# Decoder block on one core: the first normalisation's scale and offset applied to transposed tiles, the last output tile shared by three engines

## The reference

```python
h = layer_norm(x, ln0_g, ln0_b)            # (x - mean) * rsqrt(var + eps) * g + b
proj = jnp.einsum('bsd,dn->bsn', h, w_in[i])
...
h = layer_norm(DEEPNORM_ALPHA * h + mix, ln1_g[i], ln1_b[i])
...
h = layer_norm(DEEPNORM_ALPHA * h + ff + ple, ln2_g[i], ln2_b[i])
```

## Time and profile before

| what | value |
|---|---|
| median of 3 runs | 1636.98 us (1636.86 to 1637.41) |
| the profiled execution | 1637.65 us, span 1635.8 us |
| PE, PEld busy | 1588.1 us (97%), 1325.1 us (81%) |
| VectorE, ScalarE, GpSimd busy | 1150.4 (70%), 744.0 (45%), 694.2 (42%) |
| chain that ended last | PE 83%, VectorE 5%, ScalarE 4%, DMA 2%, GpSimd 2% |
| DMA | 208.51 MB, mean 127 GB/s |
| first slice of 40.9 us | PE 6 tenths, DMA 8 tenths, 295 GB/s; all later slices of PE but the last at 8 or 9 |

### The profile page before, as it was taken

One profiled execution on the slowest core, in us unless ns is written; L12 is line 12 of the kernel. 1 busy time (PEld: TensorE's weight loads), 2 busy tenths in 40 slices (PEclk: granted clock), 3 DMA queues, 4 the chain that ended last, 5 costly groups with the idle time before them and its releaser, 6 DMA issues.

```text
span 1635.8 us, 21111 instructions
## 1 busy us (share of the span) xinstructions
PE 1588.1 (97%) x7800; PEld 1325.1 (81%) x7800; DVE 1150.4 (70%) x1724; ACT 744.0 (45%) x1162; POOL 694.2 (42%) x487
## 2 busy tenths in 40 slices
PE   6999999999999999999999989999999999999996
PEld 4888888888888887888887868888888888888886
DVE  8558878437767668656336879986666579857977
ACT  3245454327888774511233644445444553433342
POOL 5222221522333145564443597765566323223334
PEclk9999999999999999999999999999999999999999
DMA  8211110101010143521333435554444598867672
GB/s 295 77 42 38 27 39 27 39 29 38 27 53 27 39 117 97 147 78 52 122 120 118 164 126 183 182 195 143 159 168 152 185 330 254 272 199 238 194 204 104
DMA packets 220693, 208.51 MB, mean 127 GB/s; under 512 B 9000, under 2 KB 190504, under 8 KB 218544
## 3 DMA queue, kind: packets, MB, share of 16 engines
q1 hardware_dynamic: 217424, 196.09, 38.7%
q10 hardware_dynamic: 3168, 11.08, 1.7%
HBM read 160.96 MB, written 46.17 MB: 127 GB/s over the span
## 4 chain that ended last, share of the span: by engine, by line
PE 83%; DVE 5%; ACT 4%; DMA 2%; POOL 2%; issue 2%; SPq 0%; DVEq 0%; ACTq 0%; POOLq 0%
PE dense L969 7%; PE dense L971 7%; PE dense L973 7%; PE dense L979 4%; PE dense L1315 3%; PE dense L1317 3%; PE dense L1316 3%; PE dense L1395 3%; PE dense L1396 3%; PE dense L1397 3%; PE mixA L1106 2%; PE dense L1047 2%; PE dense L1049 2%; PE dense L1048 2%; PE mixA L1315 2%
## 5 line engine op out<-in xcount | busy, mean ns | idle before, releaser
L969 PE MATMUL dense<-parts 128*128 128x512 f32 x528 | 183.3, 409 | 1.6 <-DVE page L2090 0.9
L943 POOL TENSOR_TENSOR parts<-page,parts 128x512 fp32r<-128x512 f32 x52 | 88.9, 1733 | 208.1 <-ACT parts L1909 208.1
L862 POOL TENSOR_TENSOR parts<-page,parts 128x512 fp32r<-128x512 f32 x108 | 156.3, 1469 | 44.9 <-ACT parts L1788 41.6
L971 PE MATMUL dense<-parts 128*128 128x512 f32 x528 | 174.0, 391 | 0.0
L973 PE MATMUL dense<-parts 128*128 128x512 f32 x528 | 173.3, 390 | 0.0
L854 POOL CAST parts<-page 128x1024 fp32r<-128x1024 f32 x43 | 49.3, 1145 | 287.4 <-PE dense L973 192.4
L905 POOL TENSOR_TENSOR page<-page 128x512 f32<-128x512 f32 x80 | 122.6, 1532 | 59.8 <-PE dense L1317 25.2
L913 POOL TENSOR_TENSOR parts<-page,parts 128x512 fp32r<-128x512 f32 x80 | 114.8, 1437 | 55.4 <-ACT parts L1835 50.6
L1919 ACT CAST parts<-page 128x1024 fp32r<-128x1024 f32 x56 | 58.8, 1055 | 142.8 <-DVE page L2614 123.2
L973 PEld LDWEIGHTS dense<-parts 128*128 128x128 f32 x528 | 99.1, 188 | 21.8
L971 PEld LDWEIGHTS dense<-parts 128*128 128x128 f32 x528 | 99.1, 188 | 21.0
(11 more groups left out here) (298 smaller groups left out, 4315.8 us busy)
## 6 DMA issues: line engine op xcount, KB each, us to landing
page<-in_w_ff SPq DMA_DIRECT2D x104, 512.0 KB, 6.0
page<-in_w_in SPq DMA_DIRECT2D x120, 256.0 KB, 3.2
page<-act_scratch SPq DMA_DIRECT2D x56, 512.0 KB, 5.7
act_scratch<-page SPq DMA_DIRECT2D x16, 1024.0 KB, 3.9
act_scratch<-page SPq DMA_DIRECT2D x16, 768.0 KB, 7.0
page<-in_w_o SPq DMA_DIRECT2D x32, 256.0 KB, 3.1
h_scratch<-page ACTq DMA_DIRECT2D x8, 512.0 KB, 3.5
page<-c_scratch SPq DMA_DIRECT2D x8, 512.0 KB, 5.0
```

The costliest lines, as they stand in the source:

```text
L862: ins = nc.gpsimd.tensor_tensor(R(lo, at, HALF), F(raw_page(c), at, HALF), R(hi, at, HALF).bitcast(F32), ALU.subtract)
L969: mm(o, whi, x_, start=first, stop=False)
L971: mm(o, whi, x_, start=False, stop=False)
```

## The change

Of the first normalisation, VectorE now makes only (x - mean) * root, in one pass. g and b (loaded once more as 16 rows of 128, turned by one transpose into columns) are applied by ScalarE to the transposed tile in PSUM, by eight activations of 128 columns, each with its scale and its bias column; then it waits for its own step and casts as before. GpSimd applies the rows g and b to the untransposed tile (`whole_token`, four operations of 512 columns), and only then may ScalarE issue the store to `h_scratch`; the stores stand three tiles later in ScalarE's order. Loads change queue: x tile 0 in two halves (SP and ACT), weight chunks 0, 1 and 3 on ACT's queue, tiles 1 to 7 and the two rows on SP's. The first two tiles' products are issued pass by pass in an order of their own (`first_values`). GpSimd makes tiles 0 to 5 before chunk 4, tiles 6 and 7 before chunk 6. `mixed` is scaled in place.

At the end, result tile 7 is transposed into mixA without waiting for tile 5's reader; its statistics are taken before tile 6 is centred; its left half is done by ScalarE and GpSimd and stored from ACT's queue, its right half by VectorE and stored from SP's.

```diff
-        rows2_in, AFTER_ROWS = rows_in, 32
+        rows2_in, AFTER_ROWS = rows_in, 16
...
+        x0_in, g0_in, b0_in, AFTER_X0, AFTER_B0 = c_stored, rows_in, pe_in, 16, 16
+        h_full, h_scaled, AFTER_W0_LOW = sem("h_full"), w0_split, 4
+        AFTER_IDENT = 48
...
+        def result_of(r):
+
+            return mixA if r == BY_BOTH else dense[r % 2]
...
-            sp.dma_start(F(PG_X), x_t[0]).then_inc(x_in[0], 16)
-            for c in range(C_END):
+            sp.dma_start(F(PG_X, 0, HALF), x_t[0][:, 0:HALF]).then_inc(x_in[0], 16)
+            sp.dma_start(F(PG_X + 1), x_t[1]).then_inc(x_in[1], 16)
+            for c in range(2, C_END):
+                if c == 3:
+                    continue
                 if c == C_AB:
                     for w in range(GN):
                         load_gate(w)
                 load_chunk(c)
-                if c == 3:
-                    for t in range(4, TT):
+                if c == 2:
+                    for t in range(2, TT):
                         sp.dma_start(F(PG_X + t), x_t[t]).then_inc(x_in[t], 16)
+                        if t == 2:
+                            sp.dma_start(F(PG_G0), row(ln0_g)).then_inc(g0_in, 16)
+                            sp.dma_start(F(PG_B0), row(ln0_b)).then_inc(b0_in, 16)
...
-            for r in range(TT):
+            for r in range(BY_BOTH):
                 if r in BY_ACT:
                     sp.wait_ge(fin_pool, BY_ACT.index(r) + 1)
                 else:
                     sp.wait_ge(fin_dve, BY_DVE.index(r) + 1)
                 sp.dma_start(out_t[RESULT[r]], F(PG_OUT + r % 4)).then_inc(out_stored[r % 4], 16)
+            sp.wait_ge(fin_dve, len(BY_DVE) + 1)
+            sp.dma_start(out_t[RESULT[BY_BOTH]][:, HALF:], F(PG_OUT + 3, HALF, HALF)).then_inc(out_stored[3], 16)
             for i in range(4):
-                sp.wait_ge(out_stored[i], AFTER_PW + 16 * 2)
+                sp.wait_ge(out_stored[i], AFTER_PW + 16 * (3 if i == 3 else 2))
...
+            def whole_token(t):
+                tile = lambda at: F(PG_X + t, at, HALF)
+                pool.wait_ge(h_turned, t + 1)
+                for at in (0, HALF):
+                    ins = nc.gpsimd.tensor_tensor(tile(at), tile(at), F(PG_G0, at, HALF), ALU.mult)
+                ins.then_inc(h_scaled, 1)
+                pool.wait_ge(h_scaled, AFTER_W0_LOW + t + 1)
+                for at in (0, HALF):
+                    ins = nc.gpsimd.tensor_tensor(tile(at), tile(at), F(PG_B0, at, HALF), ALU.add)
+                ins.then_inc(h_full, 1)
+
+            pool.wait_ge(g0_in, 16)
+            pool.wait_ge(b0_in, 16)
             for c in range(4, C_END):
+                for t in {4: range(0, 6), 6: range(6, TT)}.get(c, ()):
+                    whole_token(t)
...
-            for n, r in enumerate(BY_ACT):
-                o = F(PG_OUT + r % 4)
+            for n, r in enumerate((*BY_ACT, BY_BOTH)):
+                o, parts = F(PG_OUT + r % 4), (0, HALF) if r in BY_ACT else (0,)
                 pool.wait_ge(ln2_z, n + 1)
-                for at in (0, HALF):
+                for at in parts:
                     cols = slice(at, at + HALF)
                     ins = PT(o[:, cols], o[:, cols], F(PG_G2, at, HALF), ALU.mult)
                 ins.then_inc(ln2_zg, 1)
                 pool.wait_ge(ln2_zg, n + 1)
-                for at in (0, HALF):
+                for at in parts:
                     cols = slice(at, at + HALF)
                     ins = PT(o[:, cols], o[:, cols], F(PG_B2, at, HALF), ALU.add)
                 ins.then_inc(fin_pool, 1)
...
-                    if (name, t, k % 2) == ("vhg", 0, 0):
-                        pe.wait_ge(w0_split, k // 2 + 1)
...
-            pe.wait_ge(ident_in, 16)
+            pe.wait_ge(ident_in, AFTER_IDENT)
             pe.wait_ge(const_set, 2)
+            gb_turned = dense[1][:, HALF:HALF + 2 * KD]
+            nc.tensor.transpose(gb_turned, F(PG_COLS, 0, P)[0:2 * KD, :], ident[0:2 * KD, 0:2 * KD])
...
+            def first_values(t, n, ks):
+
+                j = JOB["vhg", t]
+                out1 = dense[SET[j]][:, 0:HALF]
+                x_, base = (XHI, XLO, XHI)[n], (WHI, WHI, WLO)[n]
+                for k in ks:
+                    if t == 0 and n != 1 and k % 2 == 0:
+                        pe.wait_ge((w0_hi, None, w0_split)[n], k // 2 + 1)
+                    ins = mm(out1, R(x_ + k, t * P, P), R(base + k // 2, (k % 2) * HALF, HALF),
+                             start=n == 0 and k == 0, stop=n == 2 and k == KD - 1)
+                if n == 2 and ks[-1] == KD - 1:
+                    end(ins, j)
+
+            every, early, late = range(KD), range(KD - 2), range(KD - 2, KD)
             turn_tokens(0)
-            for t in range(TT):
+            turn_tokens(1)
+            begin(JOB["vhg", 0])
+            pe.wait_ge(h_hi, 1)
+            first_values(0, 0, every)
+            pe.wait_ge(h_split, 1)
+            first_values(0, 1, every)
+            first_values(0, 2, range(0, 2))
+            begin(JOB["vhg", 1])
+            pe.wait_ge(h_hi, 2)
+            first_values(1, 0, every)
+            first_values(0, 2, range(2, 4))
+            pe.wait_ge(h_split, 2)
+            first_values(1, 1, every)
+            turn_tokens(2)
+            first_values(0, 2, range(4, 6))
+            first_values(1, 2, early)
+            first_values(0, 2, late)
+            first_values(1, 2, late)
+            for t in range(2, TT):
                 pe.wait_ge(h_split, t + 1)
                 value_job("vhg", t, (2, turn_tokens))
...
             def turn_result(r):
                 pe.wait_ge(f_out, LAST4 if r < 4 else LAST4 + 4 if r < 6 else LAST4 + 8)
-                if r - 2 in BY_ACT:
+                if r == BY_BOTH:
+                    pass
+                elif r - 2 in BY_ACT:
                     pe.wait_ge(ln2_z, BY_ACT.index(r - 2) + 1)
                 elif r - 2 in BY_DVE:
                     pe.wait_ge(fin_dve, BY_DVE.index(r - 2) + 1)
                 t = RESULT[r]
                 for k in range(KD):
-                    ins = nc.tensor.transpose(dense[r % 2][:, k * P:(k + 1) * P], F(PG_ACC[k], t * P, P), ident[:, :])
+                    ins = nc.tensor.transpose(result_of(r)[:, k * P:(k + 1) * P], F(PG_ACC[k], t * P, P), ident[:, :])
...
-            act.dma_start(F(PG_G0), row(ln0_g)).then_inc(rows_in, 16)
-            act.dma_start(F(PG_B0), row(ln0_b)).then_inc(rows_in, 16)
+            act.dma_start(F(PG_X, HALF, HALF), x_t[0][:, HALF:]).then_inc(x0_in, 16)
             act.dma_start(ident[:, :], c_ident).then_inc(ident_in, 16)
-            for t in range(1, 4):
-                act.dma_start(F(PG_X + t), x_t[t]).then_inc(x_in[t], 16)
+            for i, vec in enumerate((ln0_g, ln0_b)):
+                act.dma_start(F(PG_COLS, 0, P)[i * KD:(i + 1) * KD, :], vec.rearrange("(k n) -> k n", k=KD)).then_inc(ident_in, 16)
+            for c in (0, 1, 3):
+                for i in range(2):
+                    act.dma_start(F(PG_W0 + c, i * HALF, HALF), w_views["in"][:, 2 * c + i, C_HI:C_HI + HALF],
+                                  ).then_inc(w0_landed[c], 16)
...
             def tokens_high(t):
+                mixed = (mixA, mixB)[t % 2]
                 act.wait_ge(h_turned, t + 1)
+                if t == 0:
+                    own_step(nc.scalar.copy(gb[:, :], dense[1][:, HALF:HALF + 2 * KD]))
+                for k in range(KD):
+                    cols = mixed[:, k * P:(k + 1) * P]
+                    ins = A(cols, cols, ACT.Identity, scale=gb[:, k:k + 1], bias=gb[:, KD + k:KD + k + 1])
+                own_step(ins)
                 nc.scalar.copy(x_hi_all[:, :, t * P:(t + 1) * P],
-                               (mixA, mixB)[t % 2][:, :].rearrange("q (k n) -> q k n", k=KD)).then_inc(h_hi, 1)
+                               mixed[:, :].rearrange("q (k n) -> q k n", k=KD)).then_inc(h_hi, 1)
+
+            def store_tokens(t):
+                act.wait_ge(h_full, t + 1)
                 act.dma_start(h_scratch[t], F(PG_X + t)).then_inc(h_stored[t % 2], 16)
 
-            rstd_estimate(0)
-            for j in range(4):
+            gb = lbt[:, :, :].rearrange("q a n -> q (a n)")
+
+            def weight_high_0(j):
                 act.wait_ge(w0_landed[j], 32)
                 nc.scalar.copy(R(WHI + j), F(PG_W0 + j)).then_inc(w0_hi, 1)
-                if j == 1:
-                    tokens_high(0)
-                    rstd_estimate(1)
-            for t in range(1, TT + 1):
+
+            rstd_estimate(0)
+            weight_high_0(0)
+            rstd_estimate(1)
+            tokens_high(0)
+            weight_high_0(1)
+            rstd_estimate(2)
+            weight_high_0(2)
+            tokens_high(1)
+            weight_high_0(3)
+            rstd_estimate(3)
+            tokens_high(2)
+            for t in range(2):
+                store_values(PG_VHG, "vhg", t, 0)
+            for t in range(3, TT + 1):
                 if t + 1 < TT:
```

(70 more changed lines are left out.)

1 line of the change is left out of this document (removed).

## The result

| | median us | runs |
|---|---|---|
| before, beside it | 1637.20 | 1636.86 to 1637.95 |
| changed | 1658.61 | 1657.31 to 1662.25, 4 runs |

The ratio is 1.0138 (95% interval 1.0125 to 1.015): **slower, by 21 to 25 us**, where 12 were predicted and 1656 was the upper end of the range. The profiled execution of the changed kernel is the slowest of its runs, 1662.25 us (span 1660.5), 24.6 over the one before.

What follows compares the result with a forecast made beforehand. TensorE (PE), with work in 97% of the span, was taken as the bound. Start +3.0, loop +10.2 and end -1.2 summed to +12.0 over the median 1636.98: 1649.0 us, range 1640 to 1656.

Steps and rivals of the forecast that it cites:

- 8.37 against 6.34: PE waits 2.0 us for every tile: Token-tile loop: the chain of one turn outlasts PE's work, so tiles 3 to 7 add 10.2 us.
- 0.33 (0.11 to 0.45): ScalarE's scaling of each token tile: us per 128-column activation, with bounds; eight with drain and step wait take 2.77.
- Rival B: ScalarE's small activations overlap: at 0.13 us spacing no change, 1636.2 (10%); at 0.2 to 0.25, 1641 to 1644 (10%).
- Rival C: Added ScalarE work costs less than the loop's 0.74 us slack, deciding at 0.09 us per activation: 1630.6; 7%.
- The six waits are 2.0 us each, shorter, which speaks against: PE's waits ahead of tiles 2 to 7: being shorter than a 3.25 us gap argued against clock falls.
- Rival A: PE's clock falls in the new waits, 1.6 us per fall; three falls add 5, giving 1654; 22%.
- The start: Up to tile 2's first products: 36.8 where before 33.81, so +3.0 us, though PE's first work is 5.2 us earlier.
- At 160 KB per us the first is in by 8: Start loads: the first weight chunk moved to ScalarE's queue arrives by 8 us, the last by 14.4.
- The end: Result tile 7 shared by three engines: -1.2 us, bounds -0.5 and -2.
- they gain little more: Final stores: 256 KB each, following tile 6's 512 KB by 1.3 us, gain little beyond VectorE's earlier finish.
- covered by 4 us: After the last token store, VectorE's 6.3 us preparation ends at 91.3; its first use comes at 95.
- rival D: GpSimd is late at 1.77 us or more per operation, so ScalarE's first sigmoid slips: 1649 to 1654; 4%.

Runs made afterwards that it cites:

- experiment 4: Changed kernel plus nine unread products on PE ahead of each wait for the low part of tiles 2 to 7; 1652.03 us, ratio 1.0083.
- experiment 3: Changed kernel without ScalarE's eight scaling activations per tile, so g and b are not applied to the turned tile; 1636.33 us, ratio 0.9991.
- experiment 9: Experiment 8 with ScalarE casting weight chunk 3 before it scales tile 1; 1636.79 us, ratio 0.9998 to the kernel before.
- experiment 10: Experiment 9 with chunk 3 on SP's queue ahead of x tiles 2 to 7, rows behind x tile 3, tile 0 scaled before chunk 0's cast; 1637.32 us.
- experiment 2: Changed kernel with its last part undone (result tile 7 by VectorE alone, one store); 1660.0 us, ratio 1.0139 to the kernel before.
- experiment 1: Kernel before with only the change's new handling of result tile 7; 1636.63 us beside 1637.23, ratio 0.9993.
- experiment 8: Changed kernel with tile t+1's transposes moved ahead of PE's wait for tile t's low part; 1639.3 us, ratio 1.0014 to the kernel before.
- experiment 7: Changed kernel with only four of the eight scaling activations per tile, the other blocks left unscaled; one run, 1643.27 us.

## Why the prediction was wrong where it was

**The sign and the mechanism held.** "8.37 against 6.34: PE waits 2.0 us for every tile": with the clock held up (experiment 4) the period is 8.49. One activation takes 0.36 us start to start, where I took 0.33 (0.11 to 0.45); eight with the step wait 2.90 (44.38 to 47.28) against 2.77. Rivals B and C needed 0.13 and 0.09 and fall with it; that GpSimd's four operations a tile cost nothing here held too (experiment 3 has them all). That VectorE's shorter work is worth nothing was not tested by itself.

**The failed step: "The six waits are 2.0 us each, shorter, which speaks against".** On this ground the sum has no term for the clock, and the clock costs 6.6 us. I had one example of a fall, behind 3.25 us, and took the shorter wait as safer, with three falls as the bad case at 22%. There were six, one behind each wait, of 1.81 to 2.50 us as listed. The path from tile 2's products to f's start is 57.5 us where it was 37.35, +20.2 where the sum had 10.2. Of that 5 x (8.49 - 6.34) = 10.7 are the longer chain, and (10.05 - 8.49) x 5 = 7.8, with 1.7 for the last tile's slow products, are the falls; by the medians of experiment 4 they cost 6.6. Rival A was the true case, priced at a fair 1.6 for each fall and at half their number. Three of six had no reason of its own: the waits are alike, and in both traces with eight activations and unfilled waits the clock falls behind each of the last five. The forecast of 12.0, the falls (6.6), the start (2.7), the longer chain (0.5) and the end (0.6) come to 22.4, where 21.4 were measured.

**The start: +5.75 instead of +3.0** (39.56 against 33.81). "At 160 KB per us the first is in by 8": chunk 0's cast starts at 10.95. I gave both queues equal bytes. The queues of the changed kernel in the first 8 us, and of the kernel before (packets, MB, share of the DMA engines' time; q1 carries SP's transfers and q10 ScalarE's), look otherwise:

```profile
q1 hardware_dynamic: 655, 1.63, 56.3%
q10 hardware_dynamic: 468, 0.62, 21.4%
```

```profile
q10 hardware_dynamic: 302, 1.05, 38.6%
q1 hardware_dynamic: 362, 0.94, 36.4%
```

Before, ScalarE's queue moved rows of 4 KB beside SP's mixture of 4 and 2 KB, and the bytes came out about even. After, ScalarE's carries half of x tile 0 and weights in rows of 2 KB, and the identity in rows of 512 bytes, beside SP's mixture of 2 and 4 KB: 0.62 MB of 2.26. Behind the late chunk ScalarE scales tile 0 at 12.51 instead of 10.3, and the weight cast that PE waits for ends at 23.5, 2 us late. Experiments 9 and 10 take the start apart: the cast's place is worth 4.3 us of tile 2's start, the loads and ScalarE's order another 1.7. Part of the start is the execution's own: in experiment 2, with the same start, the clock was up from 20.2 to 23.6 and again from 27.0, here only from 29.5, and tile 2 started at 38.50 there.

**The end: about -0.6 instead of -1.2.** VectorE's last operation ends 10.16 us behind the start of its last addition of products, 11.45 before: 1.3 us earlier, as predicted. But what follows takes longer, as these rows of the changed kernel's timeline and its span of 1660.5 show:

```profile
1646.47 0.42 DVE L2793 TENSOR_TENSOR page<-mixB,page 128x256 f32<-128x256 f32 x1 [1.26 <-PE mixB L1459]
...
1655.88 0.75 DVE L2749 SCALAR_TENSOR_TENSOR page<-mixA,rstd,page 128x512 f32<-128x512 f32 x1
...
1656.66 0.33 SPq L798 DMA_DIRECT2D out_h<-page  x1
1656.77 0.35 ACTq L2076 DMA_DIRECT2D out_h<-page  x1
```

From VectorE's last end (1656.63, where SP's last issue starts) to the end of the span are 3.8 us; behind the single 512 KB store of before it was 3.2. I named "they gain little more"; they lost 0.6. In the eleven traces with the new end this stretch takes 3.4 to 4.0 us, in the two with the old one 3.2, so the end gains 0.6 to 1.1 us. The times alone don't tell it from nothing (experiment 1).

**The store chain: "covered by 4 us" was too sure.** I priced VectorE's preparation at 6.3 us behind the last store. In the changed kernel it takes 15.5: stores issued at 97.28, landed at 102.67, prepared until 112.8; the first sigmoid runs at 113.00 with its products ready since 108. PE does not wait yet, so rival D had no effect. Once the start is repaired, the same chain costs PE 1.93 us and a fall in the trace of experiment 10.

**What stays open.** Where between 1.14 and 1.8 us a recurring wait starts to pull the clock down. The length of one wait does not decide by itself: single waits of 1.61, 1.64 and 1.84, and one of 2.50 in experiment 2, had no fall behind them, and the wait of 3.2 us for GpSimd, which all thirteen traces have between 638 and 667 us, comes with no fall in three (the changed kernel, experiments 2 and 8), with one of 3.4 us in eight, and with one of 6.8 us in two (experiment 1, and the four activations of experiment 7). The trace of experiment 4 has a fall at 1373 us that no other has. So single falls, of some 1.6 us each, come and go between executions, and whether all executions of the changed kernel have six in the start is not known.

## What to carry to other kernels

Before work is moved onto the engine that feeds TensorE in a loop, compare the whole chain of one turn (transposes, scaling, cast, low part, products) with TensorE's own work per turn: each microsecond past it is paid every turn, and here, from somewhere between 1.1 and 1.8 us a turn, the clock fell as well, which added 6.6 us to 14.8. Then look for what in the chain can start earlier: issuing the transposes one wait sooner took back 19 of 21 us. When a stage gets shorter, go on to the next wait in line, as the cover that it had is gone with it.

## What the runs showed of the hardware

- **Clock.** A wait of 1.81 to 1.85 us in every turn of 10 us, with PE at work for the rest, brings the granted clock to 0.50 for 3.4 us each time (10 of 10 such waits, the changed kernel and experiment 2); a wait of 1.13 to 1.17 in every turn of 7.8 us left it at 1.00 (5 of 5, six activations). The Trainium skill, "TensorE: Matmul & The Clock Gate", HAM oscillation, tells of such repeated falls where operands come late; its example waits 3 to 5 us in each turn, and here half of that was enough.
- **Work that nobody reads.** Nine unread products a turn kept the granted clock at 1.00 and made the kernel 0.4% faster (1658.61 to 1652.03).
- **ScalarE.** 128 columns with two pointer operands, in place in PSUM, take 0.36 us start to start, 1024 columns 1.18. The Trainium skill, "ScalarE: Activation LUTs", What ACT_TABLE_LOAD costs, gives 186 ns, 93 for each such operand and 0.833 an element, less 93 back to back. An estimate from these figures is 0.386 and, for one by itself, 1.225. This case's traces agree within 7%; by the rule that the prediction weighed it would be 0.41 for each.
- **Queues.** Between the two kernels ScalarE's share of the first 8 us fell from 1.05 MB against SP's 0.94 to 0.62 against 1.63, while its packets only went from 302 against 362 to 468 against 655. So the two queues seem to share by packets more than by bytes; no run changed the row length alone. The Trainium skill, "DMA: Bandwidth & Descriptors", Queues, rings and completion order, says that a DMA engine takes a packet from each queue in turn; the traces lean that way, though the packets are not equal in number, and a packet on that page holds several descriptors, so these counts test it only loosely.
- **GpSimd beside VectorE.** A VectorE cast of 128x128 to uint8 takes 0.21 us in the kernel before, where GpSimd stood still, and up to 1.3 (84.00 above) while GpSimd splits weights. The whole preparation takes 10 to 12 us, and took 3.6 in the kernel before.
